# Six low parts in the two last mixers' attention: made on GpSimd instead of VectorE

## The reference, cut to what matters

```python
proj = rms_norm_2(h, norm_mix[l]) @ w_in[l]
(hq, hf, hi, hg, nq, kc, vc, ksl, vsl, ksw, vsw, ngate) = split(proj)
o_hg = hgrn2_mixer(hq, hf, hi, hg, ...)       # gated recurrence, 4 heads of 128
o_nsa = nsa_mixer(nq, kc, vc, ksl, ...)       # compressed, selected and window attention
h = h + concat(o_hg, o_nsa) @ w_out[l]
```

## Time and profile before

| | |
|---|---|
| runs | 1298.51, 1298.52, 1299.19 us; median 1298.52 |
| span of the profiled execution | 1297.2 us |
| the fastest run above that span | 1.3 us |
| busy in the span: PE, DVE, ACT, POOL | 98%, 66%, 53%, 8% |
| granted TensorE clock | 1.000 over the whole span |

### The profile page before, as it was taken

The page is one execution under the profiler, slowest core; times in us unless marked ns, Lnnn a source line. Parts: engine busy times, 40 slices in busy tenths (PEclk is TensorE's granted clock), DMA queues, the critical chain, the costliest instruction groups (busy, mean ns, idle before and its releaser), DMA issues.

```text
span 1297.2 us, 18967 instructions
## 1 busy us (share of the span) xinstructions
PE 1265.6 (98%) x7383; PEld 1077.1 (83%) x7383; DVE 860.2 (66%) x1307; ACT 690.5 (53%) x1162; POOL 108.0 (8%) x112
## 2 busy tenths in 40 slices
PE   6999999999999999999999999999999999999998
PEld 5978888887888888888877888888888787888887
DVE  5976665657645766656777766666676867766664
ACT  6775444546565544445554555555554554555552
POOL 1102000003200400001011030000021010100000
PEclk9999999999999999999999999999999999999999
DMA  9535655455522555554651155555555423555560
GB/s 354 194 124 191 215 175 210 165 191 202 176 98 98 195 197 192 186 196 141 240 215 63 67 173 189 193 196 195 173 187 213 163 67 103 189 193 185 190 192 37
DMA packets 62329, 224.45 MB, mean 173 GB/s; under 512 B 7192, under 2 KB 7328, under 8 KB 62240
## 3 DMA queue, kind: packets, MB, share of 16 engines
q1 hardware_dynamic: 59616, 214.23, 48.5%
q0 software_dynamic: 1904, 6.82, 1.6%
q10 hardware_dynamic: 720, 2.19, 0.4%
HBM read 222.16 MB, written 1.05 MB: 172 GB/s over the span
## 4 chain that ended last, share of the span: by engine, by line
PE 86%; DVE 6%; ACT 5%; issue 2%; DMA 1%; POOL 0%; ACTq 0%; DVEq 0%; POOLq 0%
PE ps L378 18%; PE ps L325 17%; PE ps L330 16%; PE ps L329 16%; PE ps L386 8%; PE ps L490 3%; PE ps L553 2%; ACT scr L1105 1%; ACT whi L1057 1%; PE ps L376 1%; PE ps L453 1%; DVE scr L1727 1%; DVE wlo L1635 1%; PE ps L531 1%; DVE scr L2131 1%
## 5 line engine op out<-in xcount | busy, mean ns | idle before, releaser
L1635 DVE TENSOR_TENSOR wlo<-raw,whi 128x1024 fp32r<-128x1024 f32 (+1 forms) x386 | 460.1, 1213 | 239.3 <-ACT whi L1057 237.8
L1057 ACT ACTIVATE whi<-raw 128x1024 fp32r<-128x1024 f32 (+1 forms) x393 | 403.9, 1045 | 281.4 <-PE ps L378 172.9
L378 PE MATMUL ps<-XT,whi 128*128 128x512 f32 x1024 | 279.4, 394 | 0.0
L378 PEld LDWEIGHTS ps<-XT,whi 128*128 128x128 f32 x1024 | 177.2, 189 | 25.4
L325 PE MATMUL ps<-whi,HT_hi 128*128 128x512 f32 x448 | 175.4, 392 | 0.5 <-DVE HT_lo L1838 0.5
L330 PE MATMUL ps<-whi,HT_lo 128*128 128x512 f32 x448 | 174.4, 389 | 0.0
L329 PE MATMUL ps<-wlo,HT_hi 128*128 128x512 f32 x448 | 174.4, 389 | 0.0
L386 PEld LDWEIGHTS ps<-XT,wlo 128*128 128x128 f32 x896 | 137.4, 189 | 18.9
L386 PE MATMUL ps<-XT,wlo 128*128 128x256 f32 x896 | 142.5, 281 | 0.0
L325 PE MATMUL ps<-whi,XT 128*128 128x512 f32 (+1 forms) x304 | 122.5, 403 | 7.3 <-DVE wlo L1635 3.5
L330 PE MATMUL ps<-whi,XT 128*128 128x512 f32 (+1 forms) x304 | 117.1, 385 | 0.0
(11 more groups left out here) (263 smaller groups left out, 1667.3 us busy)
## 6 DMA issues: line engine op xcount, KB each, us to landing
raw<-in_w_m SPq DMA_DIRECT2D x152, 512.0 KB, 4.2
raw<-in_w_n SPq DMA_DIRECT2D x108, 512.0 KB, 4.2
raw<-in_w_c SPq DMA_DIRECT2D x48, 512.0 KB, 4.6
raw<-in_w_o SPq DMA_DIRECT2D x32, 512.0 KB, 3.5
raw<-in_w_kv SPq DMA_DIRECT2D x16, 512.0 KB, 4.6
raw<-in_w_b SPq DMA_DIRECT2D x16, 512.0 KB, 4.4
raw<-in_w_w SPq DMA_DIRECT2D x16, 512.0 KB, 4.8
raw<-in_w_a SPq DMA_DIRECT2D x12, 512.0 KB, 7.5
```

Source lines behind the costliest of these rows:

```text
L378: m = pe.matmul(outs[f][:, :], hi[:, j, at(f)], both, start=(k == 0), stop=(k == KT - 1))
L1057: act.activation(whi[:, g % NSPLIT, 0:w], raw[:, g % NRAW, 0:w], ACT.Copy).then_inc(split_hi, 1)
L1635: dve.tensor_tensor(wlo[:, g % NSPLIT, 0:w], raw[:, g % NRAW, 0:w], whi[:, g % NSPLIT, 0:w].bitcast(F32), ALU.subtract).then_inc(split_lo, 1)
```

## The change

`by_tile` gets a flag. With it, the units after its first are put on GpSimd's list (and on a second list, `woven_units`). Only the product `hi` of layers 2 and 3 sets the flag: three units per layer, six in all. GpSimd makes their low parts after the `rstd` of the queries and before `cmp_key_rows`; `norm` takes its seven units from a list without the woven ones. DVE's `splits` skips whatever is on `pool_units`, as before.

```diff
-            def by_tile(names, banks, srcs, lhs):
+            def by_tile(names, banks, srcs, lhs, pooled=False):
                 outs = [fill(n, b) for n, b in zip(names, banks)]
                 for i, src in enumerate(srcs):
-                    g, hi, lo, w = unit(src, 2)
+                    g, hi, lo, w = unit(src, 2, pooled and i > 0)
+                    if pooled and i > 0:
+                        woven_units.append(g)
...
-                    yield from by_tile([f"hi{L}.0", f"hi{L}.1"], (0, 1), [a[w][16 + u] for u in range(4)], tok(XT))
+                    yield from by_tile([f"hi{L}.0", f"hi{L}.1"], (0, 1), [a[w][16 + u] for u in range(4)], tok(XT), True)
...
+            held_units = [g for g in pool_units if g not in woven_units]
+
+            def low_part(g):
+                w = units[g].shape[1]
+                pool.wait_ge(split_hi, hi_count(g))
+                pool.tensor_tensor(wlo[:, g % NSPLIT, 0:w], raw[:, g % NRAW, 0:w],
+                                   whi[:, g % NSPLIT, 0:w].bitcast(F32), ALU.subtract).then_inc(pool_lo, 1)
...
                     if tt == 0 and k in NORMS_OF_X[1:]:
-                        g = pool_units[NORMS_OF_X.index(k) - 1]
-                        w = units[g].shape[1]
-                        pool.wait_ge(split_hi, hi_count(g))
-                        pool.tensor_tensor(wlo[:, g % NSPLIT, 0:w], raw[:, g % NRAW, 0:w],
-                                           whi[:, g % NSPLIT, 0:w].bitcast(F32), ALU.subtract).then_inc(pool_lo, 1)
+                        low_part(held_units[NORMS_OF_X.index(k) - 1])
...
                 rstd(sm("cq", 16), 16, "qrstd")
+                for g in woven_units[i * len(woven_units) // 2:(i + 1) * len(woven_units) // 2]:
+                    low_part(g)
                 def cmp_key_rows():
```

More of the change, by code:

```diff
@@ L225, in program @@
         pool_units = []
+        woven_units = []
         raw_units = []
```

## The result

| | before | changed |
|---|---|---|
| device time, median of 6 runs each | 1298.51 us | 1302.82 us |
| lowest to highest | 1295.82 to 1299.92 | 1301.34 to 1307.23 |
| ratio, 95% interval | | 1.0041 [1.0031, 1.0050] |
| span of the profiled execution | 1297.2 us | 1299.8 us |

The change costs 4.3 us by the medians and 5.3 by the ratio. Predicted were 1300.1 us (+1.6) and a range up to 1302.6. The result lies just above the range, and by its interval it is slower by more than the 0.2% that held 0.86 of the chances.

The account below looks back on a forecast made before the run. PE was taken as the bound: busy in 98% of the span, 86% of the last chain. Removal 0, GpSimd's queue 0, blocking +0.81 us in each of two layers: 1298.5 + 1.6 = 1300.1 us, range 1298.2 to 1302.6.

Parts of the forecast that it names:

- the 0.2% that held 0.86 of the chances: Total time: chance 0.86 of landing within 2.6 us, what a measurement can tell from no change.
- what is removed brings nothing: DVE, hi1 to hi3 gone: 3.4 us per layer freed, but DVE then waits for ACT before hg0; 0 us.
- the 3.7 that I listed as a sign: DVE before hg0's low part: idle time of about 3.7 us, ended by ACT, would show the removal term right.
- order A: At hi0, GpSimd goes first and DVE's hi0 ends 2.23 us late; 0.81 us per layer, +1.62 in all; chance 0.42.
- order B: At hi0, DVE goes first and hi0 is on time; 0.52 us per layer, +1.04 in all; rival, chance 0.30.
- GpSimd's own queue is free: GpSimd before the compressed keys: three added low parts fit into 35.70 us of idle time; costs nothing.
- blocking, and its size: DVE and GpSimd low parts: each waits for the other to finish, with about 0.14 us of start-up overlapping.
- the slow rival: GpSimd's low part takes 3.04 us of work, not 2.27; DVE's chain 2.7 us late per layer, 1303.9 us; chance 0.10.
- The tie: Start at hi0: GpSimd asks at about 668.66, DVE begins at 668.69; GpSimd taken as first by 0.03 us.
- the absorbing of the lateness: PE after hi0: gaps of 0.94 and 0.65 us cut lateness from 2.23 to 0.64; DVE's 0.81 remains.
- predicted 0.5 to 0.7: DVE's small line, 1731 before the change: held by GpSimd's hi3, lasting 0.5 to 0.7 us instead of 0.16.
- What stays is 0.81 us per layer: PE from hi0 to 684.10: scores reach DVE 0.81 us late, and this delay stands until the end.

Follow-up runs that it names:

- vector-first run: Changed kernel, but GpSimd's first woven low part also waits until DVE has made the low part of hi0; 1299.97 us against 1297.9, ratio 1.0015.
- the second set: The changed kernel unedited, measured again in another set of five runs; 1304.23 us against 1298.51, ratio 1.0044.
- the kernel with reads beside: Kernel before, with GpSimd also subtracting two resident tiles into an unused buffer three times per layer; 1311.62 us against 1297.9, ratio 1.0105.
- hg0 after the keys: Changed kernel, but hi all on DVE and only hg0's low part on GpSimd, behind `cmp_key_rows`; 1304.91 us against 1299.08, ratio 1.0051.

## Why the prediction was right and wrong

**Right: what is removed brings nothing.** hg0 on DVE still waits for ACT, whose high part (672.56, 1.04 us) ends 0.62 us before that of the earlier trace rows, which is the layer's own shift. DVE's idle time in front of it is 1.54 us and not the 3.7 that I listed as a sign: in order A the blocked hi0 fills the difference, so that sign belonged to order B (3.74 us in the vector-first run).

**Right: GpSimd's own queue is free.** 17.52 us of cover are left; no wait of PE on line 1509.

**Right: blocking, and its size.** Low parts on GpSimd end at 670.41, 673.73 and 677.09. Put back by the 0.61 us that the layer is early, that is 671.02, 674.34 and 677.70; predicted 671.06, 674.41 and 677.76. hi0 lasts 3.41 us (3.4). The unblocked low part takes 2.36 us, where rows 8 were read as 2.27 plus start-up, 2.41. The 3.04 us of rows 8 is a blocked figure: the slow rival, which took it for work, falls with that.

**Right: order A, and by 0.03 us.** The tie was called right in both layers, with 0.42 against 0.30; at such a margin that is luck as much as reading. The vector-first run shows order B at +0.7 us per layer instead of 0.52.

**Right: the absorbing of the lateness.** The wait at the level once at 679.97 is gone, the next one is 0.36 instead of 0.65. Line 1740 takes 0.51 us in layer 3 (predicted 0.5 to 0.7). In layer 2 it takes 0.16: with the clock down PE brought its input later than GpSimd held it. The sum per layer is 0.92 to 0.95 by three stretches at full clock, against 0.81.

**Wrong: the step from "PE starts hi0 2.23 us late" to "What stays is 0.81 us per layer".** It priced PE's wait of 3.5 us, foretold almost to the digit, by its lateness alone, and took every matmul after it at its duration of before. The clock of 1.000 "over the whole span" was among the numbers before, from an execution whose longest wait there is 1.26 us; I carried it over to one whose wait is 3.45. The missing term is the fall to 1.2 GHz: 1.45 us where it came half a microsecond behind the wait and lasted 3.4 us (layer 2, profiled run), 2.5 where it came during the wait and lasted 6.8 (both layers of the second set), 0 where it stayed out (layer 3). With it the sum is 2 x 0.95 = 1.9 us without any fall and 1.9 + 2 x 2.5 = 6.9 with two, so 1300.4 to 1305.4 us from the median of before; the eleven runs lie at 1301.3 to 1307.2, with the spread that the runs of before have too (some 4 us in all). That it is the clock and not a second cost of blocking, two runs show: matmuls in front of the wait bring the changed kernel back to a ratio of 1.0017, and a stall without blocking, in the kernel before, loses the clock as well.

The Trainium skill, "TensorE: Matmul & The Clock Gate", section "What's actually happening", says that the throttled state is the default and that activity releases it, and that the number of slow matmuls varies from run to run. The runs agree with the first: overwritten matmuls in front of the wait keep the clock. The second is told there of a kernel's start; here the clock varied from run to run too, and in one run the same 3.45 us wait kept it in one layer and lost it in the other.

**Open.** What decides in a given execution whether the clock falls. Behind PE's wait of 1.26 us at hi0 it stayed at 1.00 in the profiles here; behind those of 2.54 and 3.45 us it fell in some places and not in others; behind those of 3.02, 3.82 and 6.07 us it fell in both layers of their profiles. Only one execution of each run is profiled, so no frequency is given. A run's mean clock is coarse: 0.999 is one fall of 3.4 us, or a little of the fall at the program's end. In the vector-first run, whose longest waits there are 1.26 and 1.6 us, ten of twelve executions have it, so waits below 2 us are not cleared.

## What to carry to other kernels

When a change lengthens one wait of TensorE from about one to several microseconds, price it twice: by the lateness after slack, and by the matmuls behind it at half speed, as a case with a chance of its own (here 0 to 2.8 us per wait). A relief ahead of a wait lengthens it too. Look at the longest single wait that a change creates, and at the granted clock by narrow windows: the page's tenths showed nothing of a fall of 3.4 us. A large two-input subtraction on GpSimd holds two-input VectorE operations however small, so let the one that TensorE waits for go first, and put the subtraction where the next such operation is far away.

## What I had not expected of the hardware

- A 128x16 two-input operation on DVE took 2.55 us and a 128x64 one 1.99 us (0.16 and 0.22 before) behind a GpSimd low part: the price is set by what is left of GpSimd's operation, not by DVE's size. A power of 3.81 us on GpSimd beside a large DVE operation still shows none of it.
- The fall of the clock can begin while TensorE is still idle (0.86 in the window from 669, before a wait that ended at 670.61) or 0.5 us after work has begun (672.2 in the changed kernel's layer 2). Of the ten falls at such waits in the profiles, the seven that began during the wait lasted 6.8 us, and the three that began 0.5 to 1.0 us behind it lasted 3.4. The first cost more: 2.5 to 2.8 us against 1.45.
- A start 0.03 us earlier went with being first: GpSimd in both layers of the changed kernel (668.05 against 668.08), DVE in the kernel with reads beside (668.32 against 668.35), whose first low part took its usual 1.22 us. It isn't a rule: with hg0 after the keys DVE's 128x16 operation starts at 698.33, GpSimd's low part at 698.48, and DVE is the one that is held. What settles so close a race stays open.
